# Two changes of order in a hybrid encoder layer: when probabilities are transposed in prompt attention, and where new value rows of the samples are split

## The chip, the cores and the metric

One Trainium2 chip, one core. The metric is the time of one execution of the whole program on the device, in microseconds, as the median of three executions. The kernel is written by hand, engine by engine: each engine has its own instruction list, and semaphores order what depends on each other.

## The reference

One step of a streaming encoder layer on two batches: one prompt of 2048 frames, and 8 running streams of 16 new frames with 1024 cached frames each. All arithmetic is float32. The part that matters here is the attention, with 8 heads of 64 columns and a sum F of log forget gates:

```python
def attend(q, K, V, Fq, Fk, q_pos, k_pos):
    ...
        s = jnp.einsum('bqhd,bkhd->bhqk', qblk, K, preferred_element_type=jnp.float32) * scale
        s = s + fblk[..., None] - fkT
        mask = k_pos[None, :] <= pblk[:, None]
        s = jnp.where(mask[None, None], s, -jnp.inf)
        p = jax.nn.softmax(s, axis=-1)
        return jnp.einsum('bhqk,bkhd->bqhd', p.astype(V.dtype), V)
...
def layer(x, prev_k, prev_v, prev_logf, prev_pool, prev_conv, ...):
    h = rmsnorm(x, norm_g)
    proj = jnp.einsum('btd,de->bte', h, w_in)
    ...
    K = jnp.concatenate([prev_k.astype(k.dtype), k], axis=1)
    V = jnp.concatenate([prev_v.astype(v.dtype), v], axis=1)
    o = attend(q, K, V, F[:, past:], F, q_pos, k_pos)
    b = o.reshape(B, T, D_ATT).astype(h.dtype) * jax.nn.silu(ag)
    ...
    mixed = jnp.concatenate([a, b, c.astype(h.dtype)], axis=-1)
    x_out = x + jnp.einsum('bte,ed->btd', mixed, w_out).astype(x.dtype)
```

For the prompt V is its own 2048 rows; for a stream it is 1024 cached rows and then the 16 new ones.

## The kernel before

The program has four stages: the input projection with the pool and convolution branches (0 to about 729 us), prompt attention (729 to 1165), sample attention (1165 to about 1345), and the output projection (to the end). In a split operand a float32 tile is held as a high part and a low part (the rest), and TensorE multiplies by each.

**Prompt attention (from L1247).** It goes through 8 heads, and in each through 16 steps j, one per tile of 128 queries. Tile j has j + 1 blocks of 128 keys, handled in banks of up to four blocks (`quads(j)`); two neighbouring tiles 2g and 2g + 1 form pair g. A step has as many slots n as the tile j or the tile j + 3 has banks, whichever is more. TensorE's list for a step is written out in the loop that the diff touches (`on_pe`). A slot issues:

- `turn(h, j, n)` (L1651): transposes the probabilities of a bank of tile j, up to four transposes of 128 columns. It waits for the exponentials (ScalarE, L1518) and for a free bank: the low part of two banks ago (VectorE, L1610).
- `score(h, j + 3, n)` (L1641, L1642): two matmuls of up to 512 columns for the tile three steps ahead.
- in slot 0 of an odd step, `turn_output(h, g)` (L1675): two transposes of an output that ScalarE has copied (`copy_output`, L1524).
- a share of `values` (L1667, L1668): the sum over keys for the pair before, two matmuls of 256 columns per block. Half of the pair's blocks are done in the even step, half in the odd step, spread over the slots. Block 0 starts a new sum in the output bank of two pairs ago, so it waits until VectorE has gated that output (`gate_output`, L1592).

ScalarE's list in step j is: high part of each turned bank (L1541), the exponentials of tile j + 1 behind bank 0 (L1518), and in even steps `copy_output` (L1524) behind them. VectorE's list: in each slot scores plus forget sums with their minimum for tile j + 3 (`take_chunk`, L1569), then the low part of bank n of tile j (L1610), and in odd steps `gate_output` (L1592) in slot 1. GpSimd masks, scales gates and adds parts.

TensorE's loop, cut:

```python
for n in range(slots):
    if n < n_turn:
        turn(h, j, n)
    if n < n_score:
        score(*nxt, n)
    if n == 0 and j % 2 == 1:
        ...
            turn_output(*done)
    if ended:
        values(*ended, ours[len(ours) * n // slots:len(ours) * (n + 1) // slots])
```

**Sample attention.** Stream b's 1024 cached value rows are loaded by SyncE's queue into `v_c` (L1829) and its 16 new rows into `v_n` (L1831). GpSimd makes the high part of `v_c` (L1931), then the high and the low part of `v_n` on 16 partitions (L1934, L1937); the low part of `v_c` is VectorE's (L2018, four instructions). TensorE transposes the keys of the stream (L2102, for stream b + 1 beside the scores L2121 of stream b). The queue of SyncE is in order: gates (L1876), then per stream the keys of two streams ahead (L1819, L1821, once the bank has been transposed), the values of the next one (L1829, L1831), forget sums (L1825), a store.

## Time and profile before

| | |
|---|---|
| median of 3 executions | 1520.67 us (1519.56 to 1522.1) |
| the profiled execution, its own time | 1521.51 us |
| its span | 1519.8 us |
| mean granted clock of TensorE | 0.996 |
| TensorE matmuls busy | 1475.3 us (97%) |
| VectorE, ScalarE, GpSimd busy | 893.4, 616.1, 462.2 us |

Times of rows are microseconds from the start of the span. A row of the timeline or of the chain names the engine, the source line, the tiles written and read, and how many like instructions it joins; in square brackets stands the idle time in front of it and what released it. PE is TensorE's matmul side, PEld its loading of weights, DVE VectorE, ACT ScalarE, POOL GpSimd, SPq SyncE's DMA queue. A row of busy time by stretch gives start and end, its length, then busy us and instructions of PE, PEld, DVE, ACT and POOL, TensorE's granted clock (1.00 is 2.4 GHz, 0.50 is 1.2), the DMA engines' share and GB/s. A group of instructions ends with busy us, mean ns of one, and the idle time before them with what ended it.

### The profile page before, as it was taken

The page shows a single profiled execution, that of the slowest core. Times are in us where ns is not written, and L with a number is a line of the kernel's source. Part 1 is how long each engine was busy: PE and PEld are TensorE (multiplying, and loading weights), DVE is VectorE, ACT ScalarE, POOL GpSimd, SP SyncE. Part 2 cuts the span into 40 slices and gives each one's busy share as a digit, 9 for nine tenths or more (in the row PEclk, how much of TensorE's full clock was granted, in tenths as well). Part 3 has the DMA queues.
Part 4 walks back from the last instruction along what each step waited for, and adds up shares of the span by engine and source line. Part 5 has one row for each costly group of instructions (what it writes and reads, how often), then busy time and mean ns, then how long its engine had stood idle before and what let it go on. Part 6 is the DMA issues. An engine that isn't in the chain of part 4 may idle for free.

```text
span 1519.8 us, 23891 instructions
## 1 busy us (share of the span) xinstructions
PE 1475.3 (97%) x8828; PEld 1307.8 (86%) x8828; DVE 893.4 (59%) x1979; ACT 616.1 (41%) x1307; POOL 462.2 (30%) x675
## 2 busy tenths in 40 slices
PE   8999999999999999999999999999998899999999
PEld 8997888888889999999889889888887778777887
DVE  3333103343364442411889988988996788798663
ACT  5443112131131110100678777877875444432220
POOL 2110004545530020102344454455454345303221
PEclk9999999999999999999999999999999899999999
DMA  4533124434230020160554653464333656634442
GB/s 164 159 106 100 44 76 127 156 125 139 84 105 26 27 63 25 37 149 17 125 112 69 136 125 79 106 139 101 83 116 101 223 190 211 245 131 147 161 160 91
DMA packets 179460, 173.95 MB, mean 114 GB/s; under 512 B 72271, under 2 KB 137712, under 8 KB 176272
## 3 DMA queue, kind: packets, MB, share of 16 engines
q1 hardware_dynamic: 176832, 163.44, 38.5%
q10 hardware_dynamic: 2448, 8.91, 1.5%
q8 instruction: 71, 1.16, 0.3%
q14 instruction: 45, 0.37, 0.1%
q0 software_dynamic: 64, 0.07, 0.1%
HBM read 123.27 MB, written 49.12 MB: 113 GB/s over the span
## 4 chain that ended last, share of the span: by engine, by line
PE 66%; DVE 12%; POOL 7%; issue 7%; ACT 5%; DMA 2%; DVEq 0%; SPq 0%; ACTq 0%; POOLq 0%
PE banks L1069 18%; PE banks L1063 13%; PE banks L2672 7%; PE banks L1651 6%; PE banks L1667 4%; POOL in_h_rstd L589 3%; PE banks L1668 3%; PE banks L1641 3%; PE banks L1642 3%; POOL in_out L594 3%; DVE sa_v_lo L2018 3%; ACT pa_s_ring L1518 2%; PE banks L2121 2%; PE banks L2102 2%; DVE in_out L876 1%
## 5 line engine op out<-in xcount | busy, mean ns | idle before, releaser
L1063 PE MATMUL banks<-in_w_hi,in_xt_hi 128*128 128x512 f32 (+1 forms) x680 | 243.1, 357 | 3.9 <-DVE in_w_lo L767 2.2
L1063 PE MATMUL banks<-in_w_hi,in_xt_lo 128*128 128x512 f32 (+1 forms) x680 | 237.8, 350 | 0.0
L1063 PE MATMUL banks<-in_w_lo,in_xt_hi 128*128 128x512 f32 (+1 forms) x680 | 237.2, 349 | 0.0
L1541 ACT ACTIVATE pa_pt_hi<-banks 128x512 fp32r<-128x512 f32 (+2 forms) x320 | 165.2, 537 | 89.2 <-PE banks L1651 88.9
L1610 DVE TENSOR_TENSOR pa_pt_lo<-banks,pa_pt_hi 128x512 fp32r<-128x512 f32 (+2 forms) x320 | 192.1, 605 | 15.5 <-ACT pa_pt_hi L1541 15.1
L1069 PE MATMUL banks<-in_xt_hi,in_w_hi 128*128 128x384 f32 (+1 forms) x576 | 192.4, 334 | 0.9 <-DVE in_w_lo L773 0.7
L1069 PE MATMUL banks<-in_xt_hi,in_w_lo 128*128 128x384 f32 (+1 forms) x576 | 189.3, 329 | 0.0
L1069 PE MATMUL banks<-in_xt_lo,in_w_hi 128*128 128x384 f32 (+1 forms) x576 | 189.0, 328 | 0.0
L1651 PE MATMUL banks<-ident,pa_s_ring 128*128 128x128 f32 x1088 | 174.0, 275 | 12.4 <-ACT pa_s_ring L1518 7.2
L1518 ACT ACTIVATE pa_s_ring<-pa_s_ring,pa_low 128x1024 f32<-128x1024 f32 (+2 forms) x192 | 173.2, 902 | 0.1
L1667 PE MATMUL banks<-pa_pt_hi,pa_vs 128*128 128x256 f32 x576 | 165.2, 303 | 2.4 <-DVE pa_parts L1592 1.7
L1668 PE MATMUL banks<-pa_pt_lo,pa_vs 128*128 128x256 f32 x576 | 152.9, 281 | 0.0
L1063 PEld LDWEIGHTS banks<-in_w_hi,in_xt_hi 128*128 128x128 f32 x680 | 127.9, 188 | 22.6 <-DVE in_w_lo L767 3.8
L1063 PEld LDWEIGHTS banks<-in_w_hi,in_xt_lo 128*128 128x128 f32 x680 | 127.8, 188 | 18.3
L1651 PEld LDWEIGHTS banks<-ident,pa_s_ring 128*128 128x128 f32 x1088 | 123.6, 140 | 22.5 <-ACT pa_s_ring L1518 14.0
L1063 PEld LDWEIGHTS banks<-in_w_lo,in_xt_hi 128*128 128x128 f32 x680 | 128.0, 188 | 16.7 <-issue 0.2
L1641 PE MATMUL banks<-pa_ks,pa_q_h 128*128 128x512 f32 (+2 forms) x320 | 138.0, 432 | 0.5 <-ACT in_gate_c L712 0.5
L1445 POOL TENSOR_TENSOR pa_f_diag<-pa_f_b,pa_mask_w 128x128 f32<-128x128 f32 (+3 forms) x128 | 111.9, 876 | 49.7 <-DMA pa_f_b<-scratch_f 27.7
L1667 PEld LDWEIGHTS banks<-pa_pt_hi,pa_vs 128*128 128x128 f32 x576 | 108.8, 189 | 18.6 <-DVE pa_parts L1592 12.4
L1642 PE MATMUL banks<-pa_ks,pa_q_l 128*128 128x512 f32 (+2 forms) x320 | 116.5, 365 | 0.0
L1668 PEld LDWEIGHTS banks<-pa_pt_lo,pa_vs 128*128 128x128 f32 x576 | 109.3, 190 | 6.2
L1069 PEld LDWEIGHTS banks<-in_xt_hi,in_w_hi 128*128 128x128 f32 x576 | 108.1, 188 | 3.5 <-issue 1.6
(292 smaller groups left out, 2860.5 us busy)
## 6 DMA issues: line engine op xcount, KB each, us to landing
sa_k_c<-in_cache_k_dram SPq DMA_DIRECT2D x8, 2048.0 KB, 9.2
sa_v_c<-in_cache_v_dram SPq DMA_DIRECT2D x8, 2048.0 KB, 8.2
out_dram<-in_out SPq DMA_DIRECT2D x34, 256.0 KB, 2.1
out_dram<-op_x ACTq DMA_DIRECT2D x17, 512.0 KB, 3.3
scratch_qk_t<-in_t_hi SPq DMA_DIRECT2D x32, 256.0 KB, 2.6
scratch_qk_t<-in_t_lo SPq DMA_DIRECT2D x32, 256.0 KB, 3.0
pa_q_l<-scratch_qk_t SPq DMA_DIRECT2D x16, 512.0 KB, 13.3
pa_ks<-scratch_qk_t SPq DMA_DIRECT2D x16, 512.0 KB, 6.3
```

Of the source, the lines that this page charges most:

```text
L1063: mm = pe.matmul(ps[:, u % NBANK, 0:n], tile_of(xa, t)[:, k, :], wa[:, k, c0:c0 + n], start=(k == 0 and q == 0), stop=(k == KT - 1 and q = ...
L1069: mm = pe.matmul(ps[:, u % NBANK, 0:chunk_tokens(c)], wa[:, k, c0:c0 + P], xa[c][:, k, :], start=(k == 0 and q == 0), stop=(k == KT - 1 an ...
L1445: pool.tensor_tensor(f_diag[:, n % NFD, 0:nb * P], f_b[h % 2][:, b * P:(b + nb) * P], mask_w[:, (4 - nb) * P:4 * P], ALU.add).then_inc(con ...
L1518: act.activation(sc, sc, ACT.Exp, bias=lowest, scale=-1.0, accum_out=rsum[:, h % 2, j, c:c + 1]).then_inc(exp_done, 1)
L1541: act.activation(pt_hi[g % 2][:, b:b + nb, (j % 2) * P:(j % 2 + 1) * P], ps_t[:, turn_use(h, j, n) % 3, 0:nb * P].rearrange("p (b q) -> p ...
L1610: dve.tensor_tensor(pt_lo[g % 2][:, b:b + nb, cols], ps_t[:, turn_use(h, j, n) % 3, 0:nb * P].rearrange("p (b q) -> p b q", q=P), pt_hi[g ...
L1641: pe.matmul(out, q_h[h % 2][:, j * P:(j + 1) * P], keys, start=True, stop=False)
L1642: pe.matmul(out, q_l[h % 2][:, j * P:(j + 1) * P], keys, start=False, stop=True).then_inc(scored, 1)
L1651: mm = pe.transpose(ps_t[:, to, k * P:(k + 1) * P], scores_of(j)[:, (b + k) * P:(b + k + 1) * P], ident[:, :])
L1667: pe.matmul(ps_o[g % 2][:, 0:2 * P], v, pt_hi[g % 2][:, k, :], start=(k == 0), stop=False)
L1668: mm = pe.matmul(ps_o[g % 2][:, 0:2 * P], v, pt_lo[g % 2][:, k, :], start=False, stop=(k == 2 * g + 1))
L2672: mm = pe.matmul(ring(pair, i), ma[:, n, :], wa[:, n, :], start=(n == 0 and q == 0), stop=(n == NM - 1 and q == 2))
```

## The change

Two edits. In prompt attention `turn(h, j, n)` goes from the first to the last place of each slot. In sample attention the new value rows of all streams are loaded at once as one tile of 128 partitions (16 rows for each of 8 streams) and split once into high and low halves by four GpSimd instructions behind the first `v_hi`; three DMAs per stream (`place_new_v`) then copy that stream's rows to their place in `v_hi` and `v_lo`, within SBUF. GpSimd's two instructions per stream on 16 partitions go.

```diff
--- before.py
+++ after.py
@@ -1691,8 +1691,6 @@
                     half = ended[1] + 1
                     ours = list(range(half * (j % 2), half * (j % 2 + 1)))
                 for n in range(slots):
-                    if n < n_turn:
-                        turn(h, j, n)
                     if n < n_score:
                         score(*nxt, n)
                     if n == 0 and j % 2 == 1:
@@ -1701,6 +1699,8 @@
                             turn_output(*done)
                     if ended:
                         values(*ended, ours[len(ours) * n // slots:len(ours) * (n + 1) // slots])
+                    if n < n_turn:
+                        turn(h, j, n)
         turn_output(H - 1, NG - 2)
         values(H - 1, NG - 1, range(2 * NG))
 
@@ -1771,6 +1771,8 @@
     v_hi = [m.at(n, f"v_hi{n}", [P, TC + 1, DA], F32R) for n in (136320, 173184)]
     v_lo = [m.at(n, f"v_lo{n}", [P, TC + 1, DA], F32R) for n in (154752, 191616)]
     v_n = m.at(210048, "v_n", [P, DA])
+    v_n_lo = m.at(210048, "v_n_lo", [P, DA], F32R)
+    v_n_hi = [m.at(n, f"v_n_hi{n}", [P, DA // 2], F32R) for n in (47616, 72192)]
     ps_k = m.banks(0, 2)
     ps_s = [m.banks(n, n + 1)[:, 0, :] for n in (2, 4, 5)]
     ps_o = m.banks(3, 4)[:, 0, :]
@@ -1790,8 +1792,8 @@
     kt_h = m.sem("kt_hi_done")
     kt_l = m.sem("kt_lo_done")
     vh_done = m.sem("v_hi_done")
-    vn_h = m.sem("v_new_hi_done")
-    vn_done = m.sem("v_new_lo_done")
+    vn_split = m.sem("v_new_split")
+    vn_in = m.sem("v_new_halves_placed")
     vl_done = m.sem("v_lo_done")
     scored = m.sem("chunk_scored")
     chunk_min = m.sem("chunk_min")
@@ -1828,7 +1830,18 @@
         def load_v(b):
             sp.dma_start(v_c[:, :, :],
                          cache_v[b * PAST:(b + 1) * PAST, :].rearrange("(t p) d -> p t d", p=P)).then_inc(v_in, 16)
-            sp.dma_start(v_n[0:NQ, :], new_v[b * NQ:(b + 1) * NQ, :]).then_inc(v_in, 16)
+
+        def place_new_v(b):
+            if b:
+                sp.wait_ge(vn_in, 48 * b)
+            if b >= 2:
+                sp.wait_ge(pv_done, b - 1)
+            rows = slice(b * NQ, (b + 1) * NQ)
+            for n in range(2):
+                cols = slice(n * DA // 2, (n + 1) * DA // 2)
+                sp.dma_start(v_hi[b % 2][0:NQ, TC, cols].bitcast(F32),
+                             v_n_hi[n][rows, :].bitcast(F32)).then_inc(vn_in, 16)
+            sp.dma_start(v_lo[b % 2][0:NQ, TC, :].bitcast(F32), v_n_lo[rows, :].bitcast(F32)).then_inc(vn_in, 16)
 
         def store(b, par):
             sp.wait_ge(o_done, b + 1)
@@ -1848,6 +1861,7 @@
             return
         if step == "rings_dead":
             load_v(0)
+            sp.dma_start(v_n[:, :], new_v).then_inc(v_in, 16)
             return
 
         def body(b, par):
@@ -1857,13 +1871,14 @@
                 load_k(b + 2, par)
             if b + 1 < NB:
 
-                sp.wait_ge(vn_done, b + 1)
                 sp.wait_ge(vl_done, 4 * (b + 1))
                 load_v(b + 1)
             if b + 2 < NB:
 
                 sp.wait_ge(scored, (b + 1) * NC_)
                 load_f(b + 2, par)
+            if b + 1 < NB:
+                place_new_v(b + 1)
             if b >= NB - 2:
 
                 sp.wait_ge(k_turned, (b + 1) * KB)
@@ -1875,6 +1890,8 @@
         for b in range(NB):
             sp.dma_start(q_in[:, b * HD:(b + 1) * HD],
                          by_head(gate_all, b)).then_inc(o_stored[b] if b < 2 else gates_in, 16)
+        sp.wait_ge(vn_split, 3)
+        place_new_v(0)
         for b in range(NB):
             body(b, b % 2)
         weights(2)
@@ -1925,18 +1942,22 @@
                 pool.wait_ge(qz_done, 2 * b + half + 1)
 
         def split_v_hi(b, par):
-            pool.wait_ge(v_in, 32 * (b + 1))
-
+            pool.wait_ge(v_in, 16 * (b + 2))
             wait_some(pool, pv_done, b - 1)
             pool.tensor_scalar(v_hi[par][:, 0:TC, :], v_c[:, :, :], 1.0, 0.0, ALU.mult,
                                ALU.add).then_inc(vh_done, 1)
-            pool.wait_ge(vh_done, b + 1)
-            pool.tensor_scalar(v_hi[par][0:NQ, TC, :], v_n[0:NQ, :], 1.0, 0.0, ALU.mult,
-                               ALU.add).then_inc(vn_h, 1)
-            pool.wait_ge(vn_h, b + 1)
-            pool.tensor_tensor(v_lo[par][0:NQ, TC, :], v_n[0:NQ, :],
-                               v_hi[par][0:NQ, TC, :].bitcast(F32), ALU.subtract).then_inc(vn_done, 1)
-            pool.wait_ge(vn_done, b + 1)
+
+        def split_new_v():
+            pool.wait_ge(v_in, 32)
+            prompt.stores_landed(pool)
+            for n in range(2):
+                pool.tensor_scalar(v_n_hi[n][:, :], v_n[:, n * DA // 2:(n + 1) * DA // 2], 1.0, 0.0, ALU.mult,
+                                   ALU.add).then_inc(vn_split, 1)
+            pool.wait_ge(vn_split, 2)
+            for n in range(2):
+                cols = slice(n * DA // 2, (n + 1) * DA // 2)
+                done = pool.tensor_tensor(v_n_lo[:, cols], v_n[:, cols], v_n_hi[n][:, :].bitcast(F32), ALU.subtract)
+            done.then_inc(vn_split, 1)
 
         pool.wait_ge(q_copied, 1)
         pool.wait_ge(made, 14)
@@ -1946,6 +1967,8 @@
             if b + 1 < NB:
                 lay_q(b + 1, 1 - b % 2)
             split_v_hi(b, b % 2)
+            if b == 0:
+                split_new_v()
 
     def k_banks(b, c):
 
@@ -2142,7 +2165,7 @@
 
             wait_some(pe, out_step, 5 * (b - 1) + 4)
             pe.wait_ge(vl_done, 4 * b + 4)
-            pe.wait_ge(vn_done, b + 1)
+            pe.wait_ge(vn_in, 48 * (b + 1))
             for n, tiles in enumerate(PB):
                 pe.wait_ge(p_l, b * 3 + n + 1)
                 for t in tiles:
@@ -2191,7 +2214,7 @@
     def rows_split(eng):
 
         eng.wait_ge(vl_done, 4 * NB)
-        eng.wait_ge(vn_done, NB)
+        eng.wait_ge(vn_in, 48 * NB)
 
     def own_rows_summed(eng):
```

The engines' lists show what moved. On TensorE in the second head (h = 1), the end of step 7 and the start of step 8, before (`pa_s_ring_147` holds probabilities of tile 7, `pa_s_ring_144` those of tile 8; `pa_pt_hi_148` pair 2, `pa_pt_hi_149` pair 3):

```order
L1641 MATMUL banks<-pa_ks_133,pa_q_h_129 128x384 [waits pa_chunk_with_f_and_min]
L1642 MATMUL banks<-pa_ks_133,pa_q_l_131 128x384
L1667 MATMUL banks<-pa_pt_hi_148,pa_vs_143 128x256 [waits pa_p_lo_done]
L1668 MATMUL banks<-pa_pt_lo_150,pa_vs_143 128x256
L1667 MATMUL banks<-pa_pt_hi_148,pa_vs_143 128x256 [waits pa_corner_zeroed]
L1668 MATMUL banks<-pa_pt_lo_150,pa_vs_143 128x256
L1651 MATMUL banks<-ident,pa_s_ring_144 128x128 [waits pa_p_lo_done,pa_chunk_exp]
L1651 MATMUL banks<-ident,pa_s_ring_144 128x128 x3
L1641 MATMUL banks<-pa_ks_133,pa_q_h_129 128x512 [waits pa_chunk_with_f_and_min]
L1642 MATMUL banks<-pa_ks_133,pa_q_l_131 128x512
L1667 MATMUL banks<-pa_pt_hi_149,pa_vs_143 128x256 [waits pa_p_lo_done,pa_output_gated]
L1668 MATMUL banks<-pa_pt_lo_151,pa_vs_143 128x256
```

The same place in the changed kernel:

```order
L1641 MATMUL banks<-pa_ks_133,pa_q_h_129 128x384 [waits pa_chunk_with_f_and_min]
L1642 MATMUL banks<-pa_ks_133,pa_q_l_131 128x384
L1667 MATMUL banks<-pa_pt_hi_148,pa_vs_143 128x256 [waits pa_p_lo_done]
L1668 MATMUL banks<-pa_pt_lo_150,pa_vs_143 128x256
L1667 MATMUL banks<-pa_pt_hi_148,pa_vs_143 128x256 [waits pa_corner_zeroed]
L1668 MATMUL banks<-pa_pt_lo_150,pa_vs_143 128x256
L1641 MATMUL banks<-pa_ks_133,pa_q_h_129 128x512 [waits pa_chunk_with_f_and_min]
L1642 MATMUL banks<-pa_ks_133,pa_q_l_131 128x512
L1667 MATMUL banks<-pa_pt_hi_149,pa_vs_143 128x256 [waits pa_p_lo_done,pa_output_gated]
L1668 MATMUL banks<-pa_pt_lo_151,pa_vs_143 128x256
L1651 MATMUL banks<-ident,pa_s_ring_144 128x128 [waits pa_p_lo_done,pa_chunk_exp]
L1651 MATMUL banks<-ident,pa_s_ring_144 128x128 x3
```

Before, the turn of tile 8 stands in front of the block that waits for `pa_output_gated`; now that block, with its wait, stands in front of the turn.

TensorE again, the start of step 7 in the same head, before:

```order
L1651 MATMUL banks<-ident,pa_s_ring_147 128x128 [waits pa_p_lo_done,pa_chunk_exp]
L1651 MATMUL banks<-ident,pa_s_ring_147 128x128 x3
L1641 MATMUL banks<-pa_ks_133,pa_q_h_129 128x512 [waits pa_chunk_with_f_and_min]
L1642 MATMUL banks<-pa_ks_133,pa_q_l_131 128x512
L1675 MATMUL banks<-ident,pa_o_t 128x128 [waits pa_output_copied]
L1675 MATMUL banks<-ident,pa_o_t 128x128
L1667 MATMUL banks<-pa_pt_hi_148,pa_vs_143 128x256
L1668 MATMUL banks<-pa_pt_lo_150,pa_vs_143 128x256
```

and in the changed kernel:

```order
L1641 MATMUL banks<-pa_ks_133,pa_q_h_129 128x512 [waits pa_chunk_with_f_and_min]
L1642 MATMUL banks<-pa_ks_133,pa_q_l_131 128x512
L1675 MATMUL banks<-ident,pa_o_t 128x128 [waits pa_output_copied]
L1675 MATMUL banks<-ident,pa_o_t 128x128
L1667 MATMUL banks<-pa_pt_hi_148,pa_vs_143 128x256
L1668 MATMUL banks<-pa_pt_lo_150,pa_vs_143 128x256
L1651 MATMUL banks<-ident,pa_s_ring_147 128x128 [waits pa_p_lo_done,pa_chunk_exp]
L1651 MATMUL banks<-ident,pa_s_ring_147 128x128 x3
```

The transposes of the output, with their wait for `pa_output_copied`, and the step's first share of values were behind the turn of tile 7 and are now in front of it.

SyncE's queue at the start of sample attention in the changed kernel (of before it goes from L1876 x7 straight to the keys, L1819; the changed kernel's lines are numbered otherwise):

```order
L1891 DMA sa_q_in<-scratch_gate 128x1x64 [waits sa_q_transposed]
L1891 DMA sa_q_in<-scratch_gate 128x1x64 x7
L1842 DMA sa_v_hi_182<-sa_v_n_hi_188 16x256 [waits sa_v_new_split]
L1842 DMA sa_v_hi_182<-sa_v_n_hi_189 16x256
L1844 DMA sa_v_lo_184<-sa_v_n_lo 16x512
L1821 DMA sa_k_c_154<-in_cache_k_dram 128x8x512 [waits sa_k_bank_transposed]
L1823 DMA sa_k_c_154<-out_dram 16x512
```

Three DMAs and a wait for the split now stand in front of the load of stream 2's keys.

## Rows read from the trace of the kernel before

**Rows 1.** Busy time in stretches: prompt attention as a whole (columns named above).

```profile
729.00:1165.00 436.00, 419.05 (x3018) 378.79 (x3018) 390.20 (x1128) 340.84 (x772) 206.31 (x408) 1.00 0.50 106
```

**Rows 2.** Waits in 729 to 1165: us in total, times, longest.

```profile
PEld banks L1651 <- ACT pa_s_ring L1518: 14.0, 28, 0.9
PEld banks L1667 <- DVE pa_parts L1592: 12.4, 23, 0.6
```

**Rows 3.** TensorE's timeline in one head: first turn of tiles 0, 2 to 8.

```profile
996.68 0.27 PE L1651 MATMUL banks<-ident,pa_s_ring 128*128 128x128 f32 x1
...
1002.22 0.49 PE L1651 MATMUL banks<-ident,pa_s_ring 128*128 128x128 f32 x3
...
1004.05 0.66 PE L1651 MATMUL banks<-ident,pa_s_ring 128*128 128x128 f32 x4 [0.41 <-ACT pa_s_ring L1518]
...
1006.26 0.66 PE L1651 MATMUL banks<-ident,pa_s_ring 128*128 128x128 f32 x4 [0.29 <-ACT pa_s_ring L1518]
...
1008.59 0.65 PE L1651 MATMUL banks<-ident,pa_s_ring 128*128 128x128 f32 x4
...
1011.15 0.60 PE L1651 MATMUL banks<-ident,pa_s_ring 128*128 128x128 f32 x4
...
1014.28 0.60 PE L1651 MATMUL banks<-ident,pa_s_ring 128*128 128x128 f32 x4
...
1017.39 0.60 PE L1651 MATMUL banks<-ident,pa_s_ring 128*128 128x128 f32 x4
```

**Rows 4.** ScalarE's timeline in that head: output copies of steps 0, 2, 4, 6.

```profile
997.72 0.37 ACT L1524 ACTIVATE pa_o_t<-banks 128x256 f32<-128x256 f32 x1
...
1003.90 0.37 ACT L1524 ACTIVATE pa_o_t<-banks 128x256 f32<-128x256 f32 x1
...
1008.43 0.37 ACT L1524 ACTIVATE pa_o_t<-banks 128x256 f32<-128x256 f32 x1
...
1013.47 0.37 ACT L1524 ACTIVATE pa_o_t<-banks 128x256 f32<-128x256 f32 x1
```

**Rows 5.** VectorE's timeline in that head: gating in steps 3, 5, 7.

```profile
1006.97 0.42 DVE L1592 TENSOR_TENSOR pa_parts<-banks,pa_gr 128x256 f32<-128x256 f32 x1
...
1011.96 0.41 DVE L1592 TENSOR_TENSOR pa_parts<-banks,pa_gr 128x256 f32<-128x256 f32 x1
...
1018.03 0.41 DVE L1592 TENSOR_TENSOR pa_parts<-banks,pa_gr 128x256 f32<-128x256 f32 x1
```

**Rows 6.** The chain that ended last, a stretch where TensorE leads: start, us on the chain.

```profile
961.25 0.23 PE banks L1641
...
961.72 0.22 PE banks L1675 x2
961.93 0.12 PE banks L1667
```

**Rows 7.** Sample attention, low parts of values on VectorE: the group, then two streams.

```profile
L2018 DVE TENSOR_TENSOR sa_v_lo<-sa_v_c,sa_v_hi 128x1024 fp32r<-128x1024 f32 x32 | 44.0, 1433 | 2.6 <-POOL sa_v_hi L1931 2.6
...
1224.55 4.62 DVE L2018 TENSOR_TENSOR sa_v_lo<-sa_v_c,sa_v_hi 128x1024 fp32r<-128x1024 f32 x4
...
1322.22 6.13 DVE L2018 TENSOR_TENSOR sa_v_lo<-sa_v_c,sa_v_hi 128x1024 fp32r<-128x1024 f32 x4 [2.01 <-POOL sa_v_hi L1931]
```

**Rows 8.** TensorE in sample attention: its longest stall, and the stretch behind it.

```profile
1210.34 0.90 PE L2102 MATMUL banks<-ident,sa_k_c 128*128 128x128 f32 x3 [1.87 <-DVE sa_kt_lo L2011]
...
1209.90:1216.30 6.40, 5.96 (x22) 5.03 (x23) 3.36 (x8) 1.99 (x4) 0.00 (x0) 0.50 1.00 353
```

**Rows 9.** Stream 0 and stream 2's keys: GpSimd's last split, the key load, its use.

```profile
1176.96 1.28 POOL L1937 TENSOR_TENSOR sa_v_lo<-sa_v_n,sa_v_hi 16x512 fp32r<-16x512 f32 x1
...
1174.87 0.37 SPq L1819 DMA_DIRECT2D sa_k_c<-in_cache_k_dram  x1
...
1192.29 0.49 PE L2102 MATMUL banks<-ident,sa_k_c 128*128 128x128 f32 x3
...
DMA to landing us min/median/max: 8.0/9.6/12.0
```

## The prediction

> **What bounds the kernel now.** I read busy time by stretch first. In prompt attention TensorE's matmul side works 419.05 of 436.00 us, VectorE 390.20, ScalarE 340.84 [rows 1]: TensorE sets the pace with some 17 us of slack, and VectorE, at nine tenths, is close behind, so that an answer TensorE asks of it rarely comes at once. Next the waits in that stretch: TensorE stands 14.0 us, in 28 waits, for the exponentials that a turn needs, and 12.4 us, in 23, for gated outputs that block 0 of `values` needs [rows 2]. The first is the wait that the change gives more time; the second is the one that it might make worse. Then TensorE's timeline through one head, with the answers of ScalarE and VectorE beside it: the reader is to see how long it is from a turn to the output copy and to the gated output behind it on the other two engines [rows 3 to 5]. For the durations of the pieces on the path I read the chain [rows 6], and for the samples VectorE's and TensorE's rows there [rows 7, 8].
>
> All sums are made against the profiled execution, 1521.5 us, which lies 0.8 above the median of the runs.
>
> **Edit 1, the turn last in each slot.** No instruction is added or removed. Within a head the cycle turn, score, values stays the same cycle; what changes is what stands between a turn and the next waits on its answers.
>
> *Even to odd step.* ScalarE takes the turned bank, makes its high part, then the exponentials of the next tile, then copies an output. `turn_output` of the odd step waits for that copy. Before, it stood behind the odd step's turn; now the turn stands behind it. So from first turn to first turn it can't take less than: turn of 2g to end of copy, 0.05 for the semaphore (my allowance; it makes 0.3 of the six loops' sum), two transposes 0.22 and, where slot 0 has a block, 2 x 0.12 [rows 6]. From rows 3 and 4:
> - T2 to T3: 1003.90 + 0.37 - 1002.22 = 2.05, + 0.27 = 2.32; before 1004.05 - 1002.22 = 1.83.
> - T4 to T5: 1008.43 + 0.37 - 1006.26 = 2.54, + 0.27 = 2.81; before 2.33.
> - T6 to T7: 1013.47 + 0.37 - 1011.15 = 2.69, + 0.27 + 0.24 = 3.20; before 3.13.
>
> *Odd to even step.* VectorE's gating in slot 1 of the odd step comes behind the low parts of that step, which need the turn. Block 0 of the even step waits for it, and now stands in front of the turn. So: turn of 2g + 1 to end of gating, 0.05, one block 0.24. From rows 3 and 5:
> - T3 to T4: 1006.97 + 0.42 - 1004.05 = 3.34, + 0.29 = 3.63; before 2.21.
> - T5 to T6: 1011.96 + 0.41 - 1008.59 = 3.78, + 0.29 = 4.07; before 2.56.
> - T7 to T8: 1018.03 + 0.41 - 1014.28 = 4.16, + 0.29 = 4.45; before 3.11.
>
> The six together 20.48 against 15.17: +5.3 us per head. Off this goes what VectorE's answers hold of its own queue: it works almost without a pause [rows 1], and a longer step lets the queue drain. No row shows by how much; the most is 0.7 in each of the three gatings, by which the score and block (2 x 0.23 + 0.24 [rows 6]) that now stand before the turn let it start on other work earlier; between nothing and that I take 0.33, 1.0 in all. Another 0.24 goes off because at T8 one block has been done that before came later.
>
> *Step 1.* The same wait for a copy: T0 to end of copy is 997.72 + 0.37 - 996.68 = 1.41; TensorE now has only the one-tile turn (0.11) and a score (2 x 0.23 [rows 6]) in between, and stands 1.41 + 0.05 - 0.57 = 0.9 longer.
>
> *Steps 10, 12, 14.* More slots lie between turn and block 0 there, but each turn comes later by a score and a block, 0.7, and the gating with it where no queue hides that. Three times 0 to 0.7; I take 0.9 in all.
>
> *What is won.* The waits for exponentials are 14.0 / 8 = 1.75 us per head [rows 2]; of them 0.41 and 0.29 stand in T3 and T4 [rows 3] and are counted in the loops. The other 1.05 are covered by a score and a block more in front of the turn, and go.
>
> Per head 5.3 - 1.0 - 0.2 + 0.9 + 0.9 - 1.05 = **+4.8**. Seven heads: +34. The first head has no pair of a head before, so step 1 and T2 to T4 cost nothing there, and its share of the waits for exponentials is gained: +2. Edit 1: **+36**. Its ends, by the same sum with all terms low or all high: +2.2 and +7.5 per head.
>
> **Edit 2, new value rows split once.** VectorE's low parts of values take 4.62 us per stream where GpSimd is idle, and 6.13 where it casts the 16 rows beside them [rows 7]; over eight streams 44.0 - 8 x 4.62 = 7.0 us. The two rows of GpSimd that are the other side of this go for seven streams (stream 0's ran before). Not every us is TensorE's: it is in front of other work for part of them. I take 5.5. Beside that, the longest stall, 1.87, ends at 1210.34 and TensorE's granted clock is 0.50, its lower level of 1.2 GHz, from 1209.90 to 1216.30 [rows 8]; a stall shorter by VectorE's 1.5 may leave the clock up, which is worth half of 6.4, 3.2. I take half of that, 1.6. **-7** in all, ends 0 and -10.
> The Trainium skill, SBUF — State Buffer, Terms, says that VectorE and GpSimd share a port pair, locked for a whole instruction, so that the loser blocks. By that rule each stream would give back both of GpSimd's instructions, of which rows 9 show one with 1.28; the trace's 1.5 for both is in the same region and is what I use.
>
> Added work: four GpSimd instructions of 256 columns behind `v_hi` of stream 0. The nearest row, 512 columns in 1.28 [rows 9], makes them 2.6 together if each half takes half as long, or 5.1 if a smaller one is no quicker, in the place where two instructions on 16 rows, 1.28 of them the last, go: nothing, or the +1 below. The three DMAs of streams 1 to 7 are asked for a whole stream ahead: nothing. Those of stream 0 stand in front of stream 2's keys: before, these were issued at 1174.87; now not before the split (1178.24 by rows 9) and three issues of 0.37 [rows 9], so at 1179.4, or 1181 with a longer split. A landing takes 9.6 in the median, 12.0 at most: 1189 to 1190.6, or 1193 at worst, against the use at 1192.29 [rows 9]. I count nothing; the far end is +1 and a fallen clock behind it, +3.
>
> **Sum.** 1521.5 + 36 - 7 = 1550.5, less 0.8 to the median: **1550 us**.
>
> **Rivals.**
> - *Faster: the answers come ahead.* Scores now stand before the turn, so `take_chunk` is done when the low part is wanted. If VectorE then runs ahead by as much as the turn was moved back, block 0 and `turn_output` wait no longer than before, and only the waits for exponentials go: 14.0 from rows 2, 7 for the samples: 1500. For it: VectorE's queue fills the space in front of its gatings. Against: the copy loops are ScalarE's, which is at 340.84 of 436 [rows 1] and starts as soon as a bank is turned. It decides from a gain of 0.7 at each gating and 0.5 at each copy. Chance 0.11.
> - *Most of it hidden.* The queue drains by the full 0.7 in each gating, and steps 10 to 14 wait for nothing: +2.2 per head, +15, less 7 to 10: 1527, 1521 to 1534. Chance 0.14.
> - *The clock falls too.* Six stalls of 0.5 to 1.5 us close together in each head; in the samples a stall of 1.87 stood in front of 6.4 us at half clock [rows 8]. If each head had one such stretch, 8 x 3.2 = +26: 1576. Against it: the stalls are shorter than that one. Chance 0.07.
> The Trainium skill, TensorE: Matmul & The Clock Gate, Part 1, describes a monitor of the array's activity that lets half of the pulses through when it sees too little; this is the rule behind the last rival, and the trace has one place with more idle time and the fall, rows 8.
> - *Edit 1 does nothing.* The engine's list shows that block 0 and the output's transposes did change places with the turn, so this is in the second rival only.
>
> **How the numbers follow.** The forecast has 0.68, the rivals 0.11, 0.14 and 0.07. The range takes in the hidden case and the forecast's ends, and leaves out the first and the third: 1521 to 1570. A measurement of this kernel tells some 0.2% (3 us) from no change. Faster by more: 0.12, the first rival and the last percent of the hidden case. Within: 0.04, the hidden case's low edge. Slower: 0.84.
>
> **What would show it.** Waits of TensorE at L1675 for L1524 and at L1667 for L1592 grow from 12.4 to some 40 us and those of L1651 for L1518 almost go; first turns T2 to T8 of a head lie 19 to 20 us apart instead of 15.2; prompt attention's 436 become about 472, 59 per head instead of 54.5. VectorE's share there falls below nine tenths. In the samples all low parts of values take about 4.62. I am wrong if a head is within 1 us of what it was: then the answers came early, and the rows of gating against the turn show it. I am wrong on the samples if 4.62 doesn't come or the stage keeps its length.

## The result, and the profile after

The changed kernel takes 1563.27 us (median of 4, 1560.36 to 1565.59) against 1520.79 before in the same runs: a ratio of 1.028, 95% interval 1.0267 to 1.0293. It is slower by 42.5 us. Forecast were 1550 and a range of 1521 to 1570: sign and mechanism came out, the size was a third too small.

The last output transposes of prompt attention (L1675) mark the end of that stage in every kernel here. Before they start at 1162.84, after at 1211.37, so prompt attention ends 48.5 us later (0.3 of it because its first scores start at 729.75 instead of 729.43), and all that is behind it takes 4.4 less (1519.8 - 1162.84 = 357.0 against 1563.9 - 1211.37 = 352.5). Busy time by stretch, first before and then after, each cut at that mark (columns as in [rows 1]):

```profile
729.00:1163.10 434.10, 417.81 (x3009) 377.79 (x3010) 388.55 (x1122) 339.96 (x770) 205.85 (x407) 1.00 0.50 107
1163.10:1343.00 179.90, 166.71 (x934) 135.74 (x933) 143.13 (x243) 77.60 (x180) 69.70 (x57) 0.97 0.60 207
```

```profile
729.00:1211.50 482.50, 427.32 (x3010) 373.35 (x3008) 392.80 (x1122) 340.06 (x771) 205.80 (x407) 1.00 0.45 96
1211.50:1392.00 180.50, 172.82 (x949) 142.53 (x949) 141.71 (x251) 77.80 (x180) 42.23 (x45) 0.94 0.62 210
```

The work is the same (VectorE 388.55 and 392.80, ScalarE 339.96 and 340.06), the time it is spread over is longer, and the granted clock in prompt attention stays at 1.00. TensorE's waits in 729 to 1163 before and 729 to 1211.5 after:

```profile
PE banks L1651 <- ACT pa_s_ring L1518: 7.2, 20, 0.6
PE banks L1651 <- DVE pa_pt_lo L1610: 3.8, 9, 0.5
PE banks L1667 <- DVE pa_parts L1592: 1.7, 8, 0.2
PE banks L1675 <- ACT pa_o_t L1524: 1.1, 2, 0.6
```

```profile
PE banks L1667 <- DVE pa_parts L1592: 33.8, 39, 1.3
PE banks L1675 <- ACT pa_o_t L1524: 18.0, 32, 1.0
PE banks L1651 <- ACT pa_s_ring L1518: 1.2, 3, 0.4
PE banks L1651 <- DVE pa_pt_lo L1610: 0.4, 1, 0.4
```

The waits at turns go from 11.0 us to 1.6, as the change wants. The two waits that now stand in front of the turn go from 2.8 to 51.8. The difference of the four sums, 51.8 + 1.6 - 13.8 = 39.6, is most of the 48.5. The rest is booked as busy time: 427.32 us of TensorE instead of 417.81, 9.5 more, for the same work. The profile gives a matmul its whole length, while in an unbroken run the next one starts before that is over. So a bracket leaves out part of what a stall costs: before T3, the first turn of tile 3, the last block starts at 1003.36 and is 0.28 long, the turn starts at 1004.05 and its bracket says 0.41, but in an unbroken run it would have started 0.12 behind the block: it is 0.57 late.

These are rows of the matmul side (PE). The 14.0 and 12.4 of [rows 2] are rows of the side that loads weights (PEld), which can stand idle while matmuls still run. In that view the waits at block 0 go from 12.4 to 52.8 and those at the output's transposes from 0.7 to 30.7. The prediction has set the one view against the other; this matters further down.

TensorE's timeline in one head, the rows that answer to [rows 3], with the waits that now precede them:

```profile
1028.30 0.27 PE L1651 MATMUL banks<-ident,pa_s_ring 128*128 128x128 f32 x1
1029.76 0.44 PE L1675 MATMUL banks<-ident,pa_o_t 128*128 128x128 f32 x2 [0.72 <-ACT pa_o_t L1524]
...
1032.86 0.49 PE L1651 MATMUL banks<-ident,pa_s_ring 128*128 128x128 f32 x3
...
1034.96 0.44 PE L1675 MATMUL banks<-ident,pa_o_t 128*128 128x128 f32 x2 [0.67 <-ACT pa_o_t L1524]
1035.24 0.60 PE L1651 MATMUL banks<-ident,pa_s_ring 128*128 128x128 f32 x4
...
1038.18 0.39 PE L1667 MATMUL banks<-pa_pt_hi,pa_vs 128*128 128x256 f32 x1 [1.30 <-DVE pa_parts L1592]
...
1038.52 0.60 PE L1651 MATMUL banks<-ident,pa_s_ring 128*128 128x128 f32 x4
...
1041.33 0.60 PE L1651 MATMUL banks<-ident,pa_s_ring 128*128 128x128 f32 x4
...
1045.11 0.60 PE L1651 MATMUL banks<-ident,pa_s_ring 128*128 128x128 f32 x4
...
1048.37 0.60 PE L1651 MATMUL banks<-ident,pa_s_ring 128*128 128x128 f32 x4
...
1052.39 0.38 PE L1667 MATMUL banks<-pa_pt_hi,pa_vs 128*128 128x256 f32 x1 [1.22 <-DVE pa_parts L1592]
...
1052.73 0.49 PE L1651 MATMUL banks<-ident,pa_s_ring 128*128 128x128 f32 x3
```

And the gating on VectorE in steps 3, 5 and 7, answering to [rows 5], then ScalarE's copies in steps 2, 4 and 6, answering to [rows 4]:

```profile
1037.70 0.42 DVE L1592 TENSOR_TENSOR pa_parts<-banks,pa_gr 128x256 f32<-128x256 f32 x1
...
1044.29 0.42 DVE L1592 TENSOR_TENSOR pa_parts<-banks,pa_gr 128x256 f32<-128x256 f32 x1
...
1051.92 0.41 DVE L1592 TENSOR_TENSOR pa_parts<-banks,pa_gr 128x256 f32<-128x256 f32 x1
...
1034.54 0.37 ACT L1524 ACTIVATE pa_o_t<-banks 128x256 f32<-128x256 f32 x1
...
1040.63 0.37 ACT L1524 ACTIVATE pa_o_t<-banks 128x256 f32<-128x256 f32 x1
...
1047.43 0.37 ACT L1524 ACTIVATE pa_o_t<-banks 128x256 f32<-128x256 f32 x1
```

Each link can be followed: the gating ends at 1038.12, block 0 starts at 1038.18, the turn at 1038.52. In the samples VectorE's low parts now take:

```profile
L2041 DVE TENSOR_TENSOR sa_v_lo<-sa_v_c,sa_v_hi 128x1024 fp32r<-128x1024 f32 x32 | 37.2, 1225 | 1.7 <-POOL sa_v_hi L1947 1.7
```

That is 6.8 less than the 44.0 of [rows 7].

### The profile page after: what moved, and what is told of

Its sections match the earlier page's. It is cut to its first block, busy times and chain, and to the rows that moved or that the text cites. A ratio compares the mean times of both kernels' runs of the same rounds, so it can differ in the third digit from the quotient of the medians.

```text
span 1563.9 us, 23891 instructions
## 1 busy us (share of the span) xinstructions
PE 1487.4 (95%) x8828; PEld 1307.7 (84%) x8828; DVE 892.7 (57%) x1979; ACT 616.1 (39%) x1307; POOL 434.2 (28%) x663
## 4 chain that ended last, share of the span: by engine, by line
PE 66%; DVE 10%; issue 8%; ACT 8%; POOL 6%; DMA 1%; DVEq 0%; ACTq 0%; POOLq 0%
PE banks L1069 18%; PE banks L1063 13%; PE banks L2695 7%; PE banks L1651 6%; PE banks L1667 4%; ACT pa_s_ring L1518 4%; POOL in_h_rstd L589 3%; PE banks L1668 3%; PE banks L2144 3%; PE banks L2174 3%; POOL in_out L594 3%; ACT pa_pt_hi L1541 2%; PE banks L2125 2%; PE banks L1641 2%; DVE pa_s_ring L1569 2%
## 5 line engine op out<-in xcount | busy, mean ns | idle before, releaser
L1667 PE MATMUL banks<-pa_pt_hi,pa_vs 128*128 128x256 f32 x576 | 168.3, 308 | 34.2 <-DVE pa_parts L1592 33.8
L1667 PEld LDWEIGHTS banks<-pa_pt_hi,pa_vs 128*128 128x128 f32 x576 | 108.6, 189 | 58.6 <-DVE pa_parts L1592 52.8
L1641 PE MATMUL banks<-pa_ks,pa_q_h 128*128 128x512 f32 (+2 forms) x320 | 138.4, 433 | 0.9 <-ACT in_gate_c L712 0.5
```

The source lines that it names most:

```text
L1641: pe.matmul(out, q_h[h % 2][:, j * P:(j + 1) * P], keys, start=True, stop=False)
L1667: pe.matmul(ps_o[g % 2][:, 0:2 * P], v, pt_hi[g % 2][:, k, :], start=(k == 0), stop=False)
```

## The experiments

All ran beside the kernel before. Where a ratio is given, it is of the medians of several runs with its 95% interval; where none is, there was one execution, and the comparison rests on that and on its trace.

**The samples' edit alone.** The changed kernel with TensorE's loop of before:

```diff
                 for n in range(slots):
+                    if n < n_turn:
+                        turn(h, j, n)
                     if n < n_score:
...
                         values(*ended, ours[len(ours) * n // slots:len(ours) * (n + 1) // slots])
-                    if n < n_turn:
-                        turn(h, j, n)
```

> The samples' edit alone, TensorE's loop of prompt attention as before. If the two edits add up, prompt attention keeps its length (last output transposes at about 1163) and the time is that of before less 4.4, the part behind prompt attention in the changed kernel: 1516. If instead TensorE's half-clock stretches (9.7 us in all before, about 19 in the changed kernel) come with the samples' edit itself, they are here again and the gain stays at 4 to 5; if they come from the idle times of the new prompt order, they are at most 10 us here and the time is near 1512.

1515.46 us against 1520.2, ratio 0.997 (0.9959 to 0.9982): a gain of 4.7. The last output transposes start at 1162.74, as before. TensorE's waits in front of the keys' transposes for their low parts go from 7.2 us in 8 waits to 2.8 in 3: the 1.87 of [rows 8] and four others are gone, the three at the start of the stage stay (1.43, 0.71, 0.71). The clock is at its lower level in these stretches of its samples:

```profile
1185.50:1195.50 10.00, 10.00 (x37) 8.36 (x36) 6.12 (x10) 2.86 (x7) 0.00 (x0) 0.51 0.92 323
1325.00:1329.00 4.00, 4.00 (x12) 3.12 (x11) 3.72 (x7) 3.26 (x5) 0.00 (x0) 0.57 0.26 96
```

The kernel before has 3.3 us at 1185.9 and 6.4 at 1209.9 [rows 8]. That is some 14 us in all instead of 10, and the gain is between 4 and 5: the longer stretches come without the new prompt order, as the second expectation had it. They don't come from the samples' edit either: the turn last alone (next), whose samples are those of before, has 10 us at the lower level behind the same stall, from 1231 to 1242. The stretch behind the stall of 1.87 is gone with the stall, as the prediction hoped; another, behind a stall that both kernels have, was longer.

**The turn last, alone.** The first hunk of the diff on the kernel before.

> The turn last in each slot, alone; new value rows split per stream as before. My theory: prompt attention takes all the loss, its last output transposes come at 1211 instead of 1163, and the time is 1520.8 + 48.5 = 1569. Rival: part of that loss belongs to the new loads or the split in the samples' edit; then under 1565.

1566.85 us; last output transposes at 1208.98, 46.1 later than before. 46.6 us above 1520.2, 2 under the 1569 of my theory and over the rival's 1565. TensorE's waits in prompt attention are those of the changed kernel to 0.1 us (33.8 and 18.0). The loss belongs to this edit, and with the samples' -4.7 the two add up to 1562.

**The turn between score and the rest.**

```diff
                 for n in range(slots):
-                    if n < n_turn:
-                        turn(h, j, n)
                     if n < n_score:
                         score(*nxt, n)
+                    if n < n_turn:
+                        turn(h, j, n)
                     if n == 0 and j % 2 == 1:
```

> Order score, turn, output transposes, values: the turn goes behind the score only, so that both waits stay behind it. My theory (the loss is the two waits that stand in front of the turn): the loops are as before or a score's 0.47 shorter in their slack, waits for exponentials at turns go down, and the time is 1512 to 1521. Rival (the turn's lateness itself starves ScalarE and VectorE): about half the loss, 1535 to 1550.

1525.34 us, ratio 1.0037 (1.0024 to 1.005): slower by 5, between the two expectations and nearer to the first. Of the 46 us 41 need the turn to be behind the output transposes and the values. The 5 are not explained: in its trace the output transposes end the stage 4.3 later (1167.12; the stage also starts 0.7 later), the profile's waits for exponentials are 6.5 instead of 7.2, for the low part 0.5 instead of 3.8, and for gating

```profile
PE banks L1667 <- DVE pa_parts L1592: 5.2, 16, 0.3
```

instead of 1.7, together 0.5 less than before. The stage itself is 3.6 longer, and 3.1 of that is booked as busy (420.69 us for 417.55): matmuls that start late by less than their own length, which no wait names. Why they do is open.

**The output copy first.** On the turn last alone, ScalarE's list:

```diff
+                if j % 2 == 0:
+                    ended = pair_ended(h, j, LAG)
+                    if ended:
+                        copy_output(*ended)
                 for n in range(max(len(banks), 2 * n_exp - 1)):
...
-                    if n == 0 and j % 2 == 0:
-                        ended = pair_ended(h, j, LAG)
-                        if ended:
-                            copy_output(*ended)
```

> Turn last, but ScalarE copies the output at the start of each even step, in front of that step's high part and exponentials. My theory: TensorE's waits at L1675 (23 us in all) go, except for what moves to the gating waits behind them; 10 to 20 us less than turn last alone, 1549 to 1559. Rival (the waits at L1675 only show a general lateness): the same idle time shows up at the next wait, and the time stays within 4 us of 1569.

1546.69 us, 20 less than the turn last alone. TensorE's waits at L1675 and L1667 in its prompt attention:

```profile
PE banks L1667 <- DVE pa_parts L1592: 35.4, 39, 1.3
PE banks L1675 <- ACT pa_o_t L1524: 1.5, 2, 1.0
```

Of the 18.0 at L1675 16.5 are gone, and only 1.6 came back at L1667. The rival falls.

**The gating first.** On the turn last alone, VectorE's list:

```diff
                     if n < n_take:
                         take_chunk(*nxt, n)
+                    if n == 0 and j % 2 == 1:
+                        ended = pair_ended(h, j - 1, LAG)
+                        if ended:
+                            gate_output(*ended)
                     if n < len(banks):
...
-                    if n == min(1, slots - 1) and j % 2 == 1:
-                        ended = pair_ended(h, j - 1, LAG)
-                        if ended:
-                            gate_output(*ended)
```

> Turn last, but VectorE gates the finished output in slot 0 of odd steps, in front of the low part of bank 0, so no longer behind an answer to this step's turn. My theory: TensorE's waits at L1667, 41 us with the turn last against 6 before, go down to under 10; time 1567 less 25 to 35: 1532 to 1542. Rival (the idle time is VectorE's and ScalarE's lateness as such, and comes back at turns and output transposes): 1555 or more.

1539.09 us, 28 less. The waits by the profile:

```profile
PE banks L1675 <- ACT pa_o_t L1524: 18.0, 32, 1.0
PE banks L1667 <- DVE pa_pt_lo L1614: 4.0, 8, 0.5
PE banks L1641 <- DVE pa_low L1569: 2.9, 8, 0.4
```

33.8 us for gating are gone; 4.0 for low parts and 2.9 for scores are new, which VectorE now does behind the gating. The copy's 18.0 are untouched: two loops, each with its own price.

**Both first, the turn last.** The two edits above together.

> Turn last with both answers taken out of the chain: ScalarE's output copy at the start of even steps and VectorE's gating in slot 0 of odd steps. My theory: neither wait depends on the turn in front of it, TensorE's idle time falls to that of before or under it (51 us in prompt attention), since the waits for exponentials are also covered: 1508 to 1520. Rival: the loops were only the first of several answers that come late; a good part stays, 1530 or more.

1519.36 us, ratio 0.9981 (0.9967 to 0.9996). The last output transposes start at 1161.75, 1.1 before those of the kernel before. All of the loss of 46.6 is taken out by moving two instructions of two other engines, with the turn still last. The clock is at its lower level for 20 us of the samples, twice as long as before, and yet all behind the mark takes 356.8 us, against 357.0 before.

**Both first, the turn first.** The same two edits on the kernel before.

> The order of before (turn first) with the same two early answers. The waits at L1667 of before (6 us by idle time between matmuls) and L1675 (1.4) go, those at turns for exponentials stay: 1512 to 1517. If it is as quick as the turn last with early answers, the turn's place is worth nothing once the two loops are cut; if that one is quicker by 5 or more, the change's idea (more time for the exponentials) has its gain.

1518.77 us, ratio 0.9977 (0.9964 to 0.999). The last output transposes start at 1162.09. Equal within the intervals: with the loops cut, the turn's place is worth nothing that these runs can tell. The waits of the two (the turn last above, the turn first below):

```profile
PE banks L1651 <- DVE pa_pt_lo L1614: 2.1, 9, 0.5
PE banks L1651 <- ACT pa_s_ring L1518: 1.2, 3, 0.4
```

```profile
PE banks L1651 <- DVE pa_pt_lo L1614: 7.5, 23, 0.7
PE banks L1651 <- ACT pa_s_ring L1518: 6.7, 19, 0.6
```

With the turn last the waits at turns are 11 us shorter, but the stage is no shorter. It ends 0.3 earlier and starts 1.2 earlier, so it is 0.8 longer: some of the idle time stands at L1667 for low parts (4.0) and at L1641 for scores (2.7), so that it is only 1.6 shorter as a whole, and 2.4 more are booked as busy (418.29 us for 415.88). The change's idea, more time for the exponentials, has no gain here.

**Stream 2's keys ahead of the placing DMAs.** On the samples' edit alone:

```diff
                 load_k(b + 2, par)
+            if b == 0:
+                sp.wait_ge(vn_split, 3)
+                place_new_v(0)
             if b + 1 < NB:
...
-        sp.wait_ge(vn_split, 3)
-        place_new_v(0)
         for b in range(NB):
             body(b, b % 2)
```

> The samples' edit alone (prompt order of before), with stream 0's three placing DMAs moved behind the load of stream 2's keys instead of in front of it. If the delayed key load costs something, this is 1 to 3 us quicker than the samples' edit alone (1515.5 in its run) and the half-clock stretch at the start of the samples is shorter; my theory, that it lands in time either way: 1514.5 to 1516.5, no difference.

1513.41 us, ratio 0.9944 (0.9927 to 0.996), 2 better than the samples' edit alone and outside my theory's range; the two intervals only touch. In the trace of the samples' edit alone the keys are issued at 1181.06, the late end of the 1179.4 to 1181 of the prediction; here at 1174.91. But neither trace names a wait of TensorE's for these keys, the stretch at half clock is as long (1184 to 1195 here), and all behind the mark takes 350.43 us against 350.76: the traces show 0.3 of the 2.

**Both first and the rows split once, the turn first.** The two early answers on the samples' edit alone.

> The order of before in prompt attention, with the early output copy and the early gating, and the new value rows split once. If the gains add (2.4 and 4.7 in their runs): 1513 to 1515. If both draw on the same idle time or on the clock of the samples, 1516 to 1519.

1515.64 us, ratio 0.9955 (0.9938 to 0.9972). 5.8 better than before. The interval holds the sum of the two gains, 7.1, as well as the 4.7 of the samples alone: the times can't tell. In the trace both are there: prompt attention is 1.4 shorter than before and the part behind it 4.4.

**The changed kernel with both first.**

> The changed kernel as it stands (turn last, rows split once) with the early output copy and the early gating. If the whole loss of the change is the two answers that stood behind the turn: 1563 less 47 to 49 = 1514 to 1516, the same as the order of before with these edits. If the two edits of the change disturb each other: 1519 or more.

1513.29 us, ratio 0.9944 (0.9924 to 0.9963): the change's loss of 42.5 has become a gain of 8, and this is 50 us quicker than the changed kernel.

**All of it, and the run before once more.** The keys first, the turn last, both early answers, the rows split once; beside it the kernel of the run before, unchanged, on the same chip.

> All together: turn last, early output copy, early gating, rows split once, and stream 0's placing DMAs behind stream 2's key load. Beside the same kernel with the placing DMAs in front (the last run). If the late key load costs the 2 us that lie between the samples' edit alone (1515.5) and the version with keys first (1513.4), this is 1.5 to 2.5 quicker than the last run. My theory: no difference, both 1513 to 1515.5.

> The changed kernel with the early output copy and the early gating once more, on the same chip as the run before: 1513 to 1515.5, equal to it within 1 us if the place of stream 2's key load is worth nothing, 1.5 to 2.5 slower if it is worth what the earlier pair suggests.

1513.93 us, ratio 0.9957 (0.9943 to 0.997), and 1515.77, ratio 0.9966 (0.9954 to 0.9978). Again 1.8 in favour of the keys first, again with intervals that overlap. Two pairs point the same way; neither settles it. The kernel with the placing DMAs in front took 1513.29 in the run before and 1515.77 here, so 2 us is what one kernel differs between runs; and behind the mark the traces of the pair are 0.4 apart, 351.8 and 352.2. The late key load's cost is not shown.

**Stage by stage.** The traces let the stages be compared without what happens elsewhere. Prompt attention is counted from its first score (L1641) to the last output transposes, the rest from there to the end; it is one execution per kernel. The last column is how long the clock was at its lower level in sample attention, to some 0.5 us.

| kernel | prompt attention | behind it | lower clock |
|---|---|---|---|
| before | 433.4 | 357.0 | 10 |
| turn last | 481.2 | 356.1 | 14 |
| turn between score and the rest | 437.0 | 356.5 | 10 |
| turn last, copy first | 459.6 | 355.0 | 14 |
| turn last, gating first | 450.9 | 357.3 | 17 |
| turn last, both first | 432.8 | 356.8 | 20 |
| turn first, both first | 432.0 | 357.9 | 20 |
| rows once | 433.5 | 350.8 | 14 |
| rows once, keys first | 433.4 | 350.4 | 10 |
| rows once, turn first, both first | 432.1 | 352.6 | 20 |
| the changed kernel | 481.6 | 352.5 | 20 |
| changed, both first | 433.0 | 351.9 | 17 |
| the same again | 432.8 | 352.2 | 17 |
| changed, both first, keys first | 432.9 | 351.8 | 17 |

With both answers early the turn first is 0.8 to 0.9 us shorter in prompt attention than the turn last, with either code of the samples. The start of the stage differs by up to 2.7 us between these traces (727.8 to 730.5), though the code in front of it is the same: that is in the times too.

## Why the prediction came out as it did

**The loops, term by term.** Forecast from first turn to first turn, and measured in the head of the rows above: T2 to T3 2.32 and 2.38; T3 to T4 3.63 and 3.28; T4 to T5 2.81 and 2.81; T5 to T6 4.07 and 3.78; T6 to T7 3.20 and 3.26; T7 to T8 4.45 and 4.36. T2 to T8 are 19.87 us apart, 4.7 more than the 15.17 before; my sum for them was 5.3 - 1.0 = 4.3. The answers' rows show both halves of each loop. From a turn to the end of the copy it is 2.05, 2.48 and 2.69 us (forecast 2.05, 2.54 and 2.69). From a turn to the end of the gating it is 2.88, 3.38 and 3.96 instead of 3.34, 3.78 and 4.16: earlier by 0.46, 0.40 and 0.20, in all 1.06, for which I had taken off 1.0 as VectorE's queue that drains. What was too short are the ways from the answer to the next turn: 0.33, 0.33 and 0.57 behind a copy, where I allowed 0.27, 0.27 and 0.51, and 0.40 behind each gating, where I allowed 0.29. That makes the 0.4.

**Step 1.** The wait there was forecast at 0.9, less 0.2 for the block that is done earlier. The profile names 0.72, at 1029.76, and from T15 over the next head's start to T2 it is 10.34 us instead of 9.54: +0.8.

**What failed is the term of what is won**, "The other 1.05 are covered by a score and a block more in front of the turn, and go." There were no other 1.05. The 14.0 us that I divided by eight are idle time of the weight-load side, and the 0.41 and 0.29 that I took off it are brackets of the matmul side. The two sides in the kernel before, first in the first head (729 to 783), then in the head of [rows 3] (996.5 to 1050.2):

```profile
PEld banks L1651 <- ACT pa_s_ring L1518: 4.2, 7, 0.9
PE banks L1651 <- ACT pa_s_ring L1518: 2.4, 6, 0.6
...
PEld banks L1651 <- ACT pa_s_ring L1518: 1.4, 3, 0.6
PE banks L1651 <- ACT pa_s_ring L1518: 0.7, 2, 0.4
```

On the matmul side, whose starts make up the head, a later head waits 0.7 us for exponentials, and this is T3's 0.41 and T4's 0.29: both stand in the loops already. The waits at turns did go (11.0 to 1.6 us in the stage), but outside the loops and the first head only 0.42 a head was there to win, a wait for a low part at T15. The first head's share was in the 14.0 too, and I took it off a second time. From T8 to T15, where the forecast had 0.9 - 1.05, nothing lost, it is 29.75 us instead of 28.93: +0.8. The loss in it was about right: the profile names gating waits of 0.20 and 0.67 in front of T10 and T14.

A later head, from T2 to T2, was 53.63 us and became 59.96: +6.3 instead of +4.8. Of the 1.5 that were missing 1.0 is this term, 0.4 the ways behind the answers, 0.1 step 1. The seven later heads lost 44.0 us, where I had 34, and the first lost 4.2, where I had 2. The mechanism was right: by the length of prompt attention the turn last costs 47.8 us, of which the early copy takes out 21.6, the early gating 30.2, and both together 48.3. So the two waits are all of the loss, and 3.5 of it is held by both.

**The samples.** The forecast of 7.0 us less on VectorE was right (6.8), and 37.2 for all low parts against 8 x 4.62 = 37.0 says that the once-only split on GpSimd took nothing from VectorE. Nor was the sharing one-sided before: GpSimd's two instructions took 0.61 and 1.28 us alone and 1.65 and 2.13 beside VectorE's (at 1201 to 1205), while VectorE lost 0.97 per stream over seven streams. That most of it is TensorE's was right as well: its waits for keys' low parts fall by 4.4, and where the clock is low for like times in the table (10 to 14 us, or 17 to 20), the part behind prompt attention is 5 to 5.5 us shorter with the rows split once. I had 5.5. The clock's +1.6 is the second term that failed, and in sign: the stretch of 6.4 went, but others grew, to 14 us in the samples' edit alone and 20 in the changed kernel, where before had 10. So the -7 became -4.7 in the medians of the samples' edit alone and -4.4 in the trace of the changed kernel. Against the profiled executions' own times, 1521.5 and 1565.6, the sum of 1550.5 misses by 15.1: 12.5 up to the end of prompt attention (36 against 48.5), 2.6 behind it.

**What a stretch at half clock costs** I had put at half its length, 3.2 for 6.4. The table doesn't bear that out: with the rows split once, 10 us more at the lower level go with 2.1 us more behind prompt attention (350.4 and 352.5), and with the code of before the four traces with 10 to 14 us average 356.1, the three with 17 to 20 average 357.3. That is about a fifth of the stretch. The changed kernel's own four executions (last section) make it an estimated third: two have 0.004 less mean clock than the other two, which is some 12 us more at the lower level, and are 4.5 us longer. Either is less than a half; why was not tried.

**The rivals.** Answers that come ahead (1500): copy and gating waits did not shrink but rose to 51.8. Mostly hidden (1527): the gating came 0.20 to 0.46 earlier behind its turn, not 0.7, and steps 10 to 14 did wait. A clock that falls in each head (1576): the granted clock is 1.00 for all of prompt attention, though TensorE is idle there up to 1.3 us at a time; it is not the cause of the 48.5. The rule that was cited for it (the Trainium skill, TensorE: Matmul & The Clock Gate, Part 1) has no case in that stage. In the samples the clock does fall to half behind idle times of TensorE, in the stretches above.

## What to carry to other kernels

When work is moved behind others in an engine's list, look not at what it waits for but at what waits for answers to it: each wait that it is moved behind becomes a loop through the other engines, and its length (turn to copy to transposes, turn to gating to block) could be read here from the trace of before to 0.06 us for ScalarE's copies, and was 0.09 to 0.35 too long for VectorE's gatings. Then look at those engines' lists: here two instructions, the copy and the gating, stood behind work they didn't need, and moving them up took out all of the 47 us; the turn behind the score only, with both in their old place, took out 41. And before a sum of waits is divided, look whose row it is and how it is spread: here the weight-load side waited twice as long as the matmul side, and a third of the matmul side's waits were the first head's.

## What was not expected of the hardware

The clock in sample attention. The same stall of 2.50 us, for the samples' probabilities, stands in front of 1184.59 in the kernel before and of 1184.51 in the samples' edit alone; behind the first the granted clock was 0.50 for 3.3 us, from 1185.9 to 1189.2, behind the second for about 10. In the changed kernel three stretches were at the lower level:

```profile
1216.30:1222.00 5.70, 5.17 (x21) 4.16 (x21) 2.36 (x5) 2.36 (x5) 0.54 (x2) 0.50 0.89 298
1236.00:1246.00 10.00, 10.00 (x38) 8.28 (x37) 6.23 (x10) 2.78 (x6) 0.00 (x0) 0.51 0.70 252
1376.00:1380.00 4.00, 4.00 (x12) 3.15 (x11) 3.71 (x7) 3.75 (x5) 0.00 (x0) 0.57 0.08 24
```

The first and the third answer to none of before, though their stalls are there too: three in front of keys' transposes at the start of the stage, of which the first two are 1.43 and 0.71 in both, and one of 1.57 near its end, behind which before has 1.00 (1331 to 1335). So the length of a low stretch can't be told from the stall in front of it.

It is not the kernel's alone either. At 8 to 12 us, in the first stage, where all kernels have the same code, the clock was low in the profile of before (first row) and not in that of the changed kernel:

```profile
8.00:12.00 4.00, 4.00 (x23) 4.00 (x22) 3.01 (x4) 2.14 (x4) 0.95 (x5) 0.57 1.05 405
8.00:12.00 4.00, 4.00 (x26) 4.00 (x25) 3.23 (x4) 2.17 (x4) 1.00 (x5) 1.00 1.04 403
```

And the mean granted clock is known for every execution. The changed kernel's four had 0.993, 0.994, 0.998 and 0.997, and took 1565.6, 1565.2, 1560.4 and 1561.4 us: two at more half clock, two at less, 4 to 5 us apart. The kernel before had 0.990 to 0.997 over its executions beside the experiments, and the one at 0.990 was its slowest, 1527.2. The profiled executions of the changed kernel and of the samples' edit alone, 0.993 and 0.994, showed the lowest mean clock of their kernels' executions, while that of the kernel before, 0.996, was among its higher ones; part of the half clock that the changed kernel seems to have gained may be this. So differences of 2 us between medians of four to seven executions can be the clock's, and those between the last versions may be.
